# The head of a two-block kernel in another order: first halves of both key blocks first, the very first in quarters

## The reference, cut to what matters

```python
def mem_attn_branch(qc, mem, mem_norm_g, w_kv):
    mn = rmsnorm(mem, mem_norm_g)          # mem: 256 x 1024
    kv = mn @ w_kv                         # w_kv: 1024 x 1024
    km, vm = jnp.split(kv, 2, axis=-1)     # keys and values, 256 x 512 each
    ...

def first_block(x, mem, norm_g, w_in, ...):
    h = rmsnorm(x, norm_g[l])
    proj = h @ w_in[l]                     # q, k, v, gates, ... of all three branches
    ...
    y_c = mem_attn_branch(qc, mem, mem_norm_g[l], w_mem_kv[l]) * jax.nn.silu(z_c)
    x = x + jnp.concatenate([y_a, y_b, y_c], axis=-1) @ w_out[l]
```

## Time and profile before

| | |
|---|---|
| median of 3 runs | 1083.07 us (1082.78 to 1084.24) |
| the profiled execution | 1084.58 us, its span 1082.8 us |
| PE busy | 1072.1 us, 99% of the span |
| DVE busy | 735.2 us, 68% |
| ACT busy | 513.4 us, 47% |
| POOL busy | 93.2 us, 9% |
| mean DMA rate | 122 GB/s, in the first 54 us 308 and 256 GB/s |
| mean granted clock of PE | 0.998 |

### The profile page before, as it was taken

How to read it: one execution, slowest core, us unless ns; L and a number is a source line. 1 busy time by engine, 2 the same in 40 slices (tenths; PEclk the granted TensorE clock), 3 DMA queues, 4 the chain that set the end, 5 groups by cost and what they waited for, 6 DMA issues and landing times.

```text
span 1082.8 us, 14020 instructions
## 1 busy us (share of the span) xinstructions
PE 1072.1 (99%) x5828; PEld 925.1 (85%) x5828; DVE 735.2 (68%) x821; ACT 513.4 (47%) x585; POOL 93.2 (9%) x106
## 2 busy tenths in 40 slices
PE   9999999999999999999999999999999999999997
PEld 8788888888888888888888888888999999888885
DVE  4778856557354555556765644588978777897987
ACT  6575642543343342234433643252565666655560
POOL 0301000000003000000100010003000000220202
PEclk9999999999999999999999999999999999999999
DMA  9847421223222722223321321272033244899861
GB/s 308 256 117 168 145 64 54 88 79 117 78 81 76 249 81 78 79 81 111 99 78 53 102 80 40 78 272 78 1 122 112 79 130 143 156 205 256 178 216 77
DMA packets 91950, 131.75 MB, mean 122 GB/s; under 512 B 4812, under 2 KB 59468, under 8 KB 91760
## 3 DMA queue, kind: packets, MB, share of 16 engines
q1 hardware_dynamic: 78288, 99.00, 28.0%
q0 software_dynamic: 13312, 31.73, 13.8%
q10 hardware_dynamic: 288, 0.13, 0.1%
HBM read 126.65 MB, written 4.20 MB: 121 GB/s over the span
## 4 chain that ended last, share of the span: by engine, by line
PE 92%; DVE 3%; DMA 2%; ACT 2%; issue 1%; POOLq 0%; SPq 0%; DVEq 0%; POOL 0%
PE bank L532 28%; PE bank L534 27%; PE bank L533 27%; PE bank L873 2%; PE bank L682 2%; DMA w_raw<-in_w_mem_kv 1%; DMA w_raw<-in_w_in 1%; PE bank L799 1%; DVE w_ff_lo L1581 1%; PE bank L779 1%; ACT w_ff_hi L1333 1%; DVE w_lo L1581 1%; PE bank L923 1%; PE bank L832 1%; PE bank L817 1%
## 5 line engine op out<-in xcount | busy, mean ns | idle before, releaser
L1581 DVE TENSOR_TENSOR w_lo<-w_raw,w_hi 128x2048 fp32r<-128x2048 f32 (+1 forms) x88 | 190.6, 2169 | 163.9 <-ACT w_hi L1110 137.5
L532 PE MATMUL bank<-act_t_hi,w_hi 128*128 128x512 f32 (+1 forms) x592 | 226.7, 383 | 0.3 <-ACT r_silu L1389 0.3
L534 PE MATMUL bank<-act_t_hi,w_lo 128*128 128x512 f32 (+1 forms) x592 | 223.8, 378 | 0.0
L533 PE MATMUL bank<-act_t_lo,w_hi 128*128 128x512 f32 (+1 forms) x592 | 223.6, 378 | 0.0
L1110 ACT ACTIVATE w_hi<-w_raw 128x2048 fp32r<-128x2048 f32 (+1 forms) x56 | 103.2, 1847 | 96.9 <-PE bank L534 88.1
L532 PEld LDWEIGHTS bank<-act_t_hi,w_hi 128*128 128x128 f32 x592 | 111.4, 188 | 20.9 <-issue 0.9
L534 PEld LDWEIGHTS bank<-act_t_hi,w_lo 128*128 128x128 f32 x592 | 111.4, 188 | 21.0
L533 PEld LDWEIGHTS bank<-act_t_lo,w_hi 128*128 128x128 f32 x592 | 111.5, 188 | 20.3 <-issue 0.2
L532 PE MATMUL bank<-w_hi,hidden_hi 128*128 128x512 f32 x216 | 84.1, 389 | 0.0
L534 PE MATMUL bank<-w_hi,hidden_lo 128*128 128x512 f32 x216 | 84.0, 389 | 0.0
L533 PE MATMUL bank<-w_lo,hidden_hi 128*128 128x512 f32 x216 | 84.0, 389 | 0.0
(11 more groups left out here) (360 smaller groups left out, 2136.4 us busy)
## 6 DMA issues: line engine op xcount, KB each, us to landing
w_raw<-in_w_in SPq DMA_DIRECT2D x42, 1024.0 KB, 5.3
w_raw<-in_w_ff POOLq DMA_DIRECT2D x16, 1024.0 KB, 14.4
w_raw<-in_w_ff SPq DMA_DIRECT2D x28, 512.0 KB, 4.2
w_raw<-in_w_ff SPq DMA_DIRECT2D x13, 1024.0 KB, 8.4
w_raw<-in_w_out SPq DMA_DIRECT2D x10, 1024.0 KB, 5.1
w_vo_sums<-in_w_in POOLq DMA_DIRECT2D x4, 1024.0 KB, 9.1
w_raw<-in_w_mem_kv SPq DMA_DIRECT2D x3, 1024.0 KB, 7.8
w_vo_sums<-in_w_in SPq DMA_DIRECT2D x3, 1024.0 KB, 5.5
```

What stands on the lines that cost most here:

```text
L532: pe.matmul(dst, lh, rh, start=start, stop=False, skip_group_check=onto)
L533: pe.matmul(dst, lh, rl, start=False, stop=False, skip_group_check=onto)
L534: return pe.matmul(dst, ll, rh, start=False, stop=stop, skip_group_check=onto)
L1581: return dve.tensor_tensor(dst, src, hi.bitcast(f32), ALU.subtract)
```

## The change

The two key blocks are multiplied in five pieces in place of four: chunks 0 and 1 of block 0, chunks 2 and 3 of block 0, chunks 0 to 3 of block 1, chunks 4 to 7 of block 0, chunks 4 to 7 of block 1. Loads and splits follow this order; the first half of block 0 and of the memory come in quarters. `load_x(0)` goes ahead of SP's first wait, and that wait asks for three early splits in place of one. Block 0 now uses banks 2 and 3, block 1 banks 0 and 1. There are 13 warm-up matmuls in place of 18. Some semaphores are merged to make room for new ones (tables with masks, `fg` with `wg2`, `ln1` with `ln2`), with wait values to match.

```diff
-WARM_UP = 18
+WARM_UP = 13
...
-                        if by_halves and j == 0 and kk == 0: pe.wait_ge(w0_lo, n + 1)
+                        if by_halves and j == 0 and kk == 0: pe.wait_ge(w0_lo, n + 2)
...
-            def km_block(n):
+            def km_part(n, k0, k1):
 
                 wh, wlo = weights(n, (WH, WL))
-                for half in range(2):
-                    if n == 0: pe.wait_ge((w_lo, w0_lo)[half], 1)
-                    if n == 1: pe.wait_ge((w0_lo, w_lo)[half], 2)
-                    for t in range(2):
-                        key = ("fm", n, t)
-                        if half == 0:
-                            take(2 * n + t, key)
-                        for k in range(KC // 2 * half, KC // 2 * (half + 1)):
-                            pe.wait_ge(mem_lo, k + 1)
...
+                if n == 0: pe.wait_ge(*{0: (w0_lo, 1), 2: (w_lo, 1), 4: (w0_lo, 3)}[k0])
+                if n == 1: pe.wait_ge(*{0: (w0_lo, 2), 4: (w_lo, 2)}[k0])
+                for t in range(2):
+                    key, b = ("fm", n, t), 2 - 2 * n + t
+                    if k0 == 0:
+                        take(b, key)
+                    for k in range(k0, k1):
+                        pe.wait_ge(mem_lo, k + 1)
...
-                elif name == "km":
-                    km_block(n)
+                elif n == 0:
+                    km_part(0, 0, 2)
+                    km_part(0, 2, 4)
+                    km_part(1, 0, 4)
+                    km_part(0, 4, 8)
+                elif n == 1:
+                    km_part(1, 4, 8)
...
-            act.wait_ge(w0_loaded, 16)
-            act.activation(WH[0][:, 0:1024], RAW[0][:, 0:1024], ACT.Copy).then_inc(w_hi, 1)
...
+            act.wait_ge(w0_loaded[0], 16)
+            act.activation(WH[0][:, 0:512], RAW[0][:, 0:512], ACT.Copy).then_inc(w0_hi, 1)
             act.wait_ge(columns_in, 16)
...
+            mem_chunks_hi(0, 2, 0)
+            act.wait_ge(w0_loaded[1], 16)
+            act.activation(WH[0][:, 512:1024], RAW[0][:, 512:1024], ACT.Copy).then_inc(w_hi, 1)
+            mem_chunks_hi(2, 4, 1)
+            act.wait_ge(w1_loaded, 16)
+            act.activation(WH[1][:, 0:1024], RAW[1][:, 0:1024], ACT.Copy).then_inc(w_half_hi, 1)
+            act.wait_ge(w_loaded[0], 16)
+            act.activation(WH[0][:, 1024:], RAW[0][:, 1024:], ACT.Copy).then_inc(w0_hi, 1)
+            mem_chunks_hi(4, 8, 2)
...
+            dve.wait_ge(w0_hi, 1)
+            lower(WL[0][:, 0:512], RAW[0][:, 0:512], WH[0][:, 0:512]).then_inc(w0_lo, 1)
+            mem_chunks_lo(0, 2)
             dve.wait_ge(w_hi, 1)
...
+            lower(WL[0][:, 512:1024], RAW[0][:, 512:1024], WH[0][:, 512:1024]).then_inc(w_lo, 1)
+            mem_chunks_lo(2, 4)
+            dve.wait_ge(w_half_hi, 1)
+            lower(WL[1][:, 0:1024], RAW[1][:, 0:1024], WH[1][:, 0:1024]).then_inc(w0_lo, 1)
+            dve.wait_ge(w0_hi, 2)
+            lower(WL[0][:, 1024:], RAW[0][:, 1024:], WH[0][:, 1024:]).then_inc(w0_lo, 1)
+            mem_chunks_lo(4, 8)
...
-            load(1, blocks[1][2])
-            sp.wait_ge(w0_lo, 1)
...
+            load_part(0, 0, 2, w0_loaded[0])
+            load_mem_t(0, 2, 0)
+            load_part(0, 2, 4, w0_loaded[1])
+            load_mem_t(2, 4, 1)
+            load_part(1, 0, 4, w1_loaded)
+            load_part(0, 4, 8, w_loaded[0])
+            load_mem_t(4, 8, 2)
+            load_part(1, 4, 8, w_loaded[1])
+            load_x(0)
+            sp.wait_ge(w0_lo, 3)
             load(2, blocks[2][2])
-            load_x(0)
             load_x(1)
             load(3, blocks[3][2])
```

More of the change, by code:

```diff
@@ L302, in two_blocks @@
         w_hi, w_lo, w_used = sem("w_hi_done"), sem("w_lo_done"), sem("w_block_used")
-        w0_loaded, w_half_hi = sem("w_block0_first_half_loaded"), sem("w_block1_to_4_first_half_hi")
-        w0_hi, w0_lo = sem("w_block0_second_half_hi"), sem("w_block0_second_half_1_to_4_first_half_lo")
+        w0_loaded, w1_loaded = [sem(f"w_block0_quarter{i}_loaded") for i in range(2)], sem("w_block1_first_half_loaded")
+        w_half_hi = sem("w_block1_to_4_first_half_hi")
+        w0_hi, w0_lo = sem("w_block0_first_quarter_and_second_half_hi"), sem("w_block0_to_4_early_parts_lo")
         own_lo = sem("w_lo_done_by_gpsimd")
@@ L318, in two_blocks @@
         bank_free = [sem(f"bank_free{b}") for b in range(8)]
-        ident_in, columns_in, tables_in, masks_in, thin_in, fg_in, wg2_in = (
-            sem(s + "_in") for s in ("ident", "columns", "tables", "masks", "thin", "fg", "wg2"))
+        ident_in, columns_in, tables_in, thin_in, fg_wg2_in = (
+            sem(s + "_in") for s in ("ident", "columns", "tables_and_masks", "thin", "fg_and_wg2"))
         thin_hi, thin_lo = sem("thin_hi"), sem("thin_lo")
@@ L325, in two_blocks @@
         x_in = [sem(f"x_in{j}") for j in range(TT)]
-        poolw_in, bv_in, ws_in, sg_in, bs_in, ln1_in, ln2_in = (sem(s + "_in") for s in
-                                                                ("poolw", "bv", "ws", "sg", "bs", "ln1", "ln2"))
+        poolw_in, bv_in, ws_in, sg_in, bs_in, ln_in = (sem(s + "_in") for s in
+                                                        ("poolw", "bv", "ws", "sg", "bs", "ln"))
         m_spilled, x1_spilled, x1_back, stored = (sem(s) for s in ("m_spilled", "x1_spilled", "x1_back", "stored"))
@@ L331, in two_blocks @@
         squared, rstd_done = sem("squares_summed"), sem("rstd_done")
-        memt_in, mem_lo = [sem(f"mem_t_in{i}") for i in range(2)], sem("mem_t_lo")
+        memt_in, mem_lo = [sem(f"mem_t_in{i}") for i in range(3)], sem("mem_t_lo")
         mem_diagonals, vm_scaled, ws_masked = (sem(s) for s in ("mem_diagonals", "vm_scaled", "w_s_masked"))
@@ L698, in mem_rows @@
                 give(last, "mem_rows")
-            def km_block(n):
+            def km_part(n, k0, k1):
                 wh, wlo = weights(n, (WH, WL))
-                for half in range(2):
-                    if n == 0: pe.wait_ge((w_lo, w0_lo)[half], 1)
-                    if n == 1: pe.wait_ge((w0_lo, w_lo)[half], 2)
-                    for t in range(2):
-                        key = ("fm", n, t)
-                        if half == 0:
-                            take(2 * n + t, key)
-                        for k in range(KC // 2 * half, KC // 2 * (half + 1)):
-                            pe.wait_ge(mem_lo, k + 1)
[L712 to L715, removed]
+                if n == 0: pe.wait_ge(*{0: (w0_lo, 1), 2: (w_lo, 1), 4: (w0_lo, 3)}[k0])
[6 more added lines that the diff above has]
+                        pe.wait_ge(mem_lo, k + 1)
+                        last = three(bank[b][:, 0:NMEM], wh[:, k, tile_of(t)], wlo[:, k, tile_of(t)], MEMH[:, k, :], MEML[:, k, :],
+                                     k == 0, k == KC - 1)
+                    if k1 == KC:
+                        give(last, key)
                 b, u = turn[key]
@@ L749, in sum_f @@
                 pe.wait_ge(ones_set, 1)
-                pe.wait_ge(tables_in, 16 * 2)
+                pe.wait_ge(tables_in, 16 * 3)
                 dst = take(6, "F")
@@ L1107, in split @@
                 c0 = w // 2 if n in (1, 2, 3, GATES) else 0
-                if c0:
+                if c0 and n != 1:
                     act.activation(WH[n % 2][:, 0:c0], RAW[n % 2][:, 0:c0], ACT.Copy).then_inc(w_half_hi, 1)
@@ L1275, in side @@
                 if n == LOW:
[L1276 removed]
+                    act.wait_ge(fg_wg2_in, 16 * (1 + STACK // THIN))
                     act.activation(WG2S[:, :], WG2[:, :], ACT.Copy).then_inc(gate2_hi, 1)
@@ L1433, in _, with mem_chunks_hi @@
             act.activation(SSUM[:, 0:1], ONES[:, 0:1], ACT.Square)
-            act.wait_ge(w0_loaded, 16)
-            act.activation(WH[0][:, 0:1024], RAW[0][:, 0:1024], ACT.Copy).then_inc(w_hi, 1)
-            act.wait_ge(columns_in, 16)
[L1437 to L1442, removed]
+            def mem_chunks_hi(c0, c1, s):
+                act.wait_ge(memt_in[s], 16)
+                for c in range(c0, c1):
+                    act.activation(MEMH[:, c, :], MEMT[:, c, :], ACT.Copy, scale=col(C_MEMN + c)).then_inc(t_hi, 1)
+            act.wait_ge(w0_loaded[0], 16)
+            act.activation(WH[0][:, 0:512], RAW[0][:, 0:512], ACT.Copy).then_inc(w0_hi, 1)
+            act.wait_ge(columns_in, 16)
+            mem_chunks_hi(0, 2, 0)
[7 more added lines that the diff above has]
+            mem_chunks_hi(4, 8, 2)
             for n in range(ff1_0):
@@ L2174, in drain @@
                 if name == "w_out" and i == 5:
-                    dve.wait_ge(fg_in, 16)
+                    dve.wait_ge(fg_wg2_in, 16 * (1 + STACK // THIN))
                     def scale(j):
@@ L2238, in drain @@
                 if name == "w_out2" and i == 3:
-                    dve.wait_ge(ln1_in, 32)
+                    dve.wait_ge(ln_in, 32)
                     r0 = MT + TT + H + 3 * TT
@@ L2264, in stage, with mem_chunks_lo @@
```

(31 more changed lines are left out.)

9 lines of the change are left out of this document (4 added, 5 removed).

## The result

| | before | changed |
|---|---|---|
| median of 8 runs each | 1083.08 us (1082.66 to 1084.24) | 1086.48 us (1084.93 to 1087.22) |
| ratio, 95% interval | | 1.0027 (1.0016 to 1.0038) |
| span of the traced execution | 1082.8 us | 1083.1 us |
| PE busy | 1072.1 us, 5828 matmuls | 1070.1 us, 5818 matmuls |

The change makes the kernel slower by 0.27%, some 3 us. The traced execution of the changed kernel is its fastest, 1084.93; the spans of the other seven are 1083.2 to 1085.4. That of the kernel before, 1084.58, stands 1.5 above its median. What the two traces show of the loss, 0.3 us between their spans, is therefore its small end.

A forecast was written before the change was run, and what follows sets the result against it. PE, busy 99% of the span, was taken as the bound, its head set by load waits. Second transposes 0.3 us earlier, other edits nothing, gave 1082.8 us against the 1083.07 median; eight in ten: 1081.6 to 1084.7.

The forecast's parts named there:

- Start of the keys, the new wait: PE's key matmuls start at 6.75, not 8.07, bounded by the warm-up; PE then waits 1.25 us for block 1.
- Block 2: Issued 1.4 us later, 5.96 from issue to landing: lands at 18.4, not 16.97; PE waits 0.7 us for it.
- third of a megabyte still to move: Data taken as still ahead of block 2 at its old issue, beside the 5.96 us to landing that was kept.
- Block 4 and G: G, start of the second group of transposes, is set by block 4's landing (30.0 to 30.4): 34.37, not 34.67.
- the term of -0.3: Start of the second transposes moves 0.3 us earlier, and everything behind it moves with it.
- Rival 2: Block 4 keeps 9.90 us from issue to landing, block 2's 1.3 us delay goes through: second transposes 36.0, total 1084.4; 24%.
- Rival 1: Block 4 lands at 29.3 and PE's own time of 33.6 starts the second transposes: -1.1, total 1082.0; 12%.
- The thin stretch of 12 to 13: DMA at 127 GB/s just after block 2's old issue; claimed to stay thin.
- the stretch of 18 to 19: DMA at 231 GB/s after block 3's issue; should fill, being short by 0.15 MB or 0.4 us.
- four DMAs more: Four extra DMAs cost SP's queue about 0.4 to 0.5 each, 2 us between 3 and 6; counted as nothing.
- From 34.67 on ... PE has work in front of it: After the second transposes start, PE has work through the rest, so that start alone in the head carries to the end.
- rival 3: Shorter warm-up plus standing still leaves the keys at 1.2 GHz: second transposes +1.2, or +4.1 and 1087.2 total; 5%.

The follow-up runs named there:

- five in block 2's wait: Changed kernel (13 warm-up matmuls) plus five extra matmuls on ones after the last piece of the keys, where PE waits for block 2: 1083.84 us, ratio 1.0002.
- 8: Changed kernel with 8 warm-up matmuls in place of 13: 1083.95 us, ratio 1.0003 to the kernel before.
- the attempt at the fastest: Changed kernel with 14 warm-up matmuls and 3 and 4 more in PE's two waits of the head: 1083.80 us, ratio 1.0004.
- the rerun: The changed kernel timed again with no edit: 1086.92 us against 1084.14 for the kernel before, ratio 1.0026.

## Why the prediction was wrong

The forecast was 1082.8, and 1086.48 was measured. It lies in the 7% given to slower by over 0.2%, but by a way that none of the rivals names.

**Start of the keys, the new wait:** 6.75 and 1.25 us at 9.75 forecast; 6.48 and 1.04 ahead of 11.22 measured. The times are near, but what bounds the start was wrong: the warm-up was over at 6.08, not 6.75, and PE waited 0.41 for the first chunk of the memory. It is the data that bounds it.

**Block 2:** 18.2 to 18.6 forecast. It landed at 17.80 in the first trace, at 18.0 and 18.5 in two others (five in block 2's wait, and 8), and at 18.9 to 19.8 in the remaining six with x ahead: from issue to landing it took either 5.1 to 5.2 us or 6.5 to 6.8. In those six PE waited 1.5 to 1.9 us for it, not 0.7, which gives back most of what the keys had won. I had one value, 5.96, between the two that occur; the spread was missing from my bounds. The "third of a megabyte still to move" beside the 5.96 was misread, too: by the prediction's own landings, 2 MB at 10.1 and 3 at 13.0, it was 0.7 MB at 11.0. The new order has as much ahead of block 2 (0.2 MB of block 1 and 0.5 of x), so keeping the value did no harm. Why there are two groups stays open.

**Block 4 and G:** 34.37 forecast. 33.64 in the first trace, 34.02 to 34.63 in the other seven with x ahead, but for the attempt at the fastest: the term of -0.3 was right in sign and measured -1.0 in the first trace and -0.04 to -0.65 in the others. Block 4 was to land between 30.0 and 30.4; it landed at 29.36, and at 29.1 to 30.0 in the others. SP's issue at 21.3 took 0.38 in place of 2.72, shorter, as I had it, but it did not last until 23, and the landing did not keep its 9.90 us:

```profile
21.30 8.05 DMA w_raw<-in_w_in
```

Rival 2 (the issue chain holds) is out. Rival 1 (PE is the bound) had block 4 at 29.3 and G at 33.6, which is the first trace's head, though a wait of 0.47 for DVE still stands there; where the transposes follow without that wait, as in the rerun, PE is the bound. G is not quite the one time that carries over either: without that wait the 16 transposes take 2.3 us and not 2.6, so the rerun is 0.2 ahead at G and 0.5 ahead behind it. The thin stretch of 12 to 13, which I had staying, is full at 394 GB/s, and the stretch of 18 to 19, as forecast, at 381. The sum counts four DMAs more; there are three, and no landing shows their 2 us. The hole is at 13 to 15 with 171:

```profile
13.00:15.00 2.00, 2.00 (x19) 2.00 (x18) 1.71 (x5) 1.51 (x3) 0.00 (x0) 1.00 0.56 171
```

**"From 34.67 on ... PE has work in front of it", and "all behind it with it":** this is the step that failed. One stage, 780 us on, has a chain from a load over DVE to PE in which DVE and PE have nothing to spare and the load about 1 us. The row of it stood in the trace of before, as a wait of PE for DVE of 0.2 us; I didn't read it, since the change touches nothing there. What it did touch is PE's instruction stream. I priced the five warm-up matmuls by their time alone and the shift of PE's later fetches at nothing. The two fetches that matter came 0.9 and 1.0 us later, the loads beside them landed up to 3 us later, and the kernel with this one difference was 4.1 us slower; the whole change, with its better head, 3 us.

**The clock (rival 3):** not with 13. With 8, PE idle for 1.75 us behind them, it came true and cost nothing. The keys' matmuls start 0.21 us apart, at 1.2 GHz, until 12.4, and 0.12 apart, at 2.4, from there, though the clock column says 1.00 for both:

```profile
11.13 0.41 PE L533 MATMUL bank<-mem_t_hi,w_hi 128*128 128x256 f32 x1
11.35 0.41 PE L534 MATMUL bank<-mem_t_lo,w_hi 128*128 128x256 f32 x1
...
12.93 0.28 PE L533 MATMUL bank<-mem_t_hi,w_hi 128*128 128x256 f32 x1
13.05 0.28 PE L534 MATMUL bank<-mem_t_lo,w_hi 128*128 128x256 f32 x1
```

It uses up the wait for block 1, which is gone: the keys end 0.9 us later than with 13, and the second transposes start at 34.30, held by block 4 (landed at 30.02) and not by PE. My price for the clock left that cover out.

## What to carry to other kernels

An edit that changes the number of PE's instructions can move its instruction fetches for the rest of the program, by steps that the count alone does not tell (13 moved them, 16 did not). Before costing such an edit at nothing, look for stages where a load is awaited with little slack, and see in the DMA view where the instruction packets fall against it. To test it, put the same number of idle instructions elsewhere: if the time comes back, it was the phase and not the edit.

## What the runs showed of the hardware that I had not expected

Near 808 a 16 KB packet of queue 8 takes 0.9 to 1.5 us when it begins 0.2 to 0.3 after the load's issue, ahead of its bytes, and 2.0 to 3.1 us when it starts with them, and the 512 KB load then lands after 5.3 to 6.5 us in place of 3.5 to 4.2. In the two slower traces (the rerun, and the kernel before with 13) the second meeting has the packet begin 2.1 to 2.2 us after the issue, amid the load's bytes; it takes 1.1 and 1.5 us, and the load still lands after 5.6 and 6.1. Each time 15 of the 16 parts are there by 3.6 to 3.8 us and one is late. That these go together, and that the time follows, holds in all thirteen traces.

Open are why a packet that starts with the load's bytes takes 2.0 us in one execution and 3.1 in another, why the fetch stands at a few places only, and why the untraced runs of the kernel before have spans from 1080.8 to 1083.4. To move the load and leave the fetch where it is was not tried; it would be the test from the other side.
